# Samples' recurrence moved from the tail into the input projection of a hybrid decoder step

## The chip, the cores and the metric

The kernel runs on one core of a Trainium2 chip. The metric is the device time of one execution in microseconds. Engines: TensorE (PE, its weight loads PEld), VectorE (DVE), ScalarE (ACT), GpSimd (POOL) and SyncE (SP), which here only issues DMAs; each has its own instruction queue and they wait for one another by semaphores. Sixteen DMA engines serve the core.

## The reference

One layer of a decoder step, in float32, for a prompt of 2048 tokens and for 8 sequences with 4 new tokens each (32 "samples"; 2080 columns in all). `h = rmsnorm(x)`, then `z = h @ w_in`, whose columns feed four mixers; their gated outputs go through `w_out` and a last RMS norm.

- A: attention with forget gates; for the samples over 64 cached pages of 128 keys per sequence.
- B: a matrix-state recurrence (RWKV-7), 4 heads of 64, followed by a group norm, a bonus and a gate.
- C: causal pooling. D: a convolution of width 31 with layer norm and a pointwise product.

The part that is moved is B's recurrence for the samples, for each of the 8 sequences from its own 64x64 state per head, four tokens one after another:

```
def rwkv7_step(s, inp):
    r_t, w_t, k_t, v_t, kk_t, a_t = inp
    s_kk = jnp.einsum('bhvk,bhk->bhv', s, kk_t)
    s = s * w_t[:, :, None, :] - s_kk[..., None] * (kk_t * a_t)[:, :, None, :] + v_t[..., None] * k_t[:, :, None, :]
    o = jnp.einsum('bhvk,bhk->bhv', s, r_t)
    return s, o
```

Behind it, for all 2080 columns: `o = ((o - mean) * rsqrt(var + GN_EPS)) * gn_g + gn_b`, plus `sum(r * k * rk) * v`, times a gate; the mean and the variance run over each head's 64 rows.

## The kernel before

Everything is laid out with channels on the 128 partitions and tokens along the free dimension. Five queues are written out by hand. The order of the work:

1. **Input projection** (lines 753 to 757 are its chunk): 25 slots of 128 output columns, each in 5 chunks of 416 tokens (`CHUNKS`, `CW`) of 8 matmuls, in PSUM banks 0 to 4. ScalarE evicts each chunk, and the slot is stored to `zT` in DRAM. Beside it VectorE and GpSimd do the mixers C and D and B's preparation, with small matmuls in banks 5 to 7. At slot 22 B's preparation is over: `smp` holds the samples' columns of r, decay, k, kk, rate and v (6 x 2 x 32 per partition), and eight DMAs (`rw_stored`) have stored the prompt's parts.
2. After slot 23 TensorE computes the **value rows** (L841, banks 5 to 7, 17 tiles), ScalarE copies them to `vtok`. Then slot 24. VectorE computes the log forget gates from `vtok` (L1757 to L1776, `nl_ready`, `nc_ready`); TensorE turns them (L738) between chunks 0, 1 and 2 of slot 24.
3. SyncE meanwhile loads `wvf`, masks, `aux` (L479 to L483) and then `kq`, `qT_s`, `kT_s` (L488 to L490) for the attention, waits for `nc_ready`, writes `ncD` and loads its broadcast. GpSimd gathers the cached forget rows into `scores_`.
4. **Prompt attention** (L895, L908, L919), until about 1153 us.
5. **Prompt's scan** (`rwkv_pair`, matmuls by the helper at L948): 8 pairs, in each of them four `key_step`s of the samples' attention, whose 16 pages of 128 KB each SyncE issues one by one (L525). Ahead of the third set of pages SyncE loads an identity `id64_s` (L541), behind it the samples' states `s_wkv` (L545).
6. **The tail.** VectorE: `s_done` comes after four steps of the samples' recurrence. Each step first spreads five of the samples' quantities (columns with channels on partitions) into block-diagonal tiles `z_exp` (L2029); TensorE multiplies each by `ones_head` (L1194), so that in PSUM every partition has the whole row of its head; then VectorE updates the state (L2034 to L2054). TensorE turns two blocks of the samples' attention probabilities per step (`turn_probs`, L738), and ScalarE copies them back (L1526). Then the **group norm**: 30 sums over heads (L1242) in the order t (channel half), c (chunk) with a `value_tile` after every third; VectorE subtracts the mean (L2068), ScalarE squares, takes logarithm and exponential for the inverse root, VectorE multiplies the bonus (L2075), and when all is there it scales (L2083) and applies gain, bonus, bias and gate over whole halves of 2080 columns (L2086, L2087, `mixb_ready` 2). A value tile is 8 small matmuls over 1 MB of cached values that GpSimd gathers (L720) into one of four slots, `v_slot`; the next gather into a slot waits for the tile that used it.
7. **Output projection** (`project`, L1257): 17 token tiles, each 2 x 8 matmuls of 512 columns, with the other 54 value tiles in between, residual and RMS norm behind.

In the group norm a wait for the loads of `g_rkk`, `g_v` and `gate_b` (`gn_in`, six DMAs of 1 MB issued when the scan is over, L558 to L561) and for `s_done` stands ahead of the first sum.

Of the kernel before, what the change touches and what calls it, by code (L numbers as in the profile page):

```python
# [11 lines left out]
P = 128  # L12
# [14 lines left out]
COL_VF, VF = 512, 260  # L27
MIX_A, MIX_B, MIX_C, MIX_D = 0, 2, 4, 6
# [21 lines left out]
CH = 64  # L50
# [35 lines left out]
def build(nc, I, O):  # L86
    ctx = ExitStack()
    with ctx:
# [7 lines left out]

        ncD = nc.dram_tensor("ncD", [4, SEQ], F32, kind="Internal").ap()
# [165 lines left out]
        dmask = area(HT + 24402, P)  # L263
# [79 lines left out]
        id64_s = area(HT + 12932, CH)  # L343
        wkv_o = area(7200, 256)[0:CH]
        s_wkv = area(15616, DEC_BATCH, 2 * 64)
        z_exp = area(0, 5, DEC_BATCH * 2 * 64)
        s_tmp = area(5120, DEC_BATCH * 2 * 64)
        s_tm2 = area(6144, DEC_BATCH * 2 * 64)
        s_kk = area(7168, 16)
# [16 lines left out]
        s_z = sem("s_z")  # L366
        s_mm2 = sem("s_mm2")
# [84 lines left out]
        def _(sp):  # L452
# [124 lines left out]
            sp.wait_ge(s_done, 1)  # L577
            for t in range(2):
                sp.dma_start(O['wkv_sample'][:, 0, 2 * t:2 * t + 2].rearrange("b h v k -> (h v) b k"),
                             s_wkv[:, :, t * 64:(t + 1) * 64]).then_inc(wkv_stored, 16)  # L580
# [8 lines left out]
            sp.wait_ge(mixb_ready, 2)  # L589
# [145 lines left out]
        def _(pe):  # L735
# [97 lines left out]
            def value_rows(n):  # L833
                r = P if n < TT else SMP
                if n == 0:
                    pe.wait_ge(pars_in, 32)
                    pe.wait_ge(lora_read, 20)
# [4 lines left out]
                last.then_inc(vf_mm, 1)  # L842

# [18 lines left out]
            for n in range(2, N_SLOTS):  # L862
# [13 lines left out]
                if n == 18:  # L876
                    loras()
                if n == 23:
# [320 lines left out]
            pe.wait_ge(D['pT'], D0['pT'] + 16)  # L1199
            pe.wait_ge(D['p'], D0['p'] + 9)  # L1200
            transpose(psum[0:SMP, 6, 0:P], s_new[:, :]).then_inc(D['pT_tr'], 1)
            pe.wait_ge(D['l_bc'], D0['l_bc'] + 1)
            nc.tensor.matmul(psum[:, 7, 0:P], l_bc[:, :], ident[:, :], start=True, stop=True).then_inc(D['l_mm'], 1)

# [22 lines left out]
            pe.wait_ge(s_done, 1)  # L1227
            pe.wait_ge(gn_in, 16 * 6)
            pe.wait_ge(D['pT'], D0['pT'] + 17)
            g = 0  # L1230
            for k, src in enumerate((o_rw, gn_sq, g_rkk)):
                for t in range(2):
                    for c in range(CHUNKS):
# [11 lines left out]
                        if g % 3 == 0:  # L1245
                            value_tile(g // 3 - 1)
# [973 lines left out]
```

## Time and profile before

| | us |
|---|---|
| median of 3 runs | 1962.89 (1961.5 to 1963.37) |
| the profiled execution | 1961.91 |
| its span in the profile | 1960.1 |
| TensorE busy | 1801.5 (92%) |
| VectorE busy | 817.9 (42%) |
| ScalarE busy | 478.5 (24%) |
| GpSimd busy | 170.1 (9%) |

The profile is one execution. Its span runs from the first to the last instruction, and the device time is 1.8 us more. Times of the rows are microseconds from the start of the span. The chain of waits is followed back from the last instruction: at each step to what released it. The granted clock is a share of TensorE's full speed, and the DMA share is the busy share of the 16 DMA engines.

### The profile page before, as it was taken

The page shows a single profiled execution, that of the slowest core. Times are in us where ns is not written, and L with a number is a line of the kernel's source. Part 1 is how long each engine was busy: PE and PEld are TensorE (multiplying, and loading weights), DVE is VectorE, ACT ScalarE, POOL GpSimd, SP SyncE. Part 2 cuts the span into 40 slices and gives each one's busy share as a digit, 9 for nine tenths or more (in the row PEclk, how much of TensorE's full clock was granted, in tenths as well). Part 3 has the DMA queues.
Part 4 walks back from the last instruction along what each step waited for, and adds up shares of the span by engine and source line. Part 5 has one row for each costly group of instructions (what it writes and reads, how often), then busy time and mean ns, then how long its engine had stood idle before and what let it go on. Part 6 is the DMA issues. An engine that isn't in the chain of part 4 may idle for free.

```text
span 1960.1 us, 34623 instructions
## 1 busy us (share of the span) xinstructions
PE 1801.5 (92%) x14642; PEld 1092.4 (56%) x14642; DVE 817.9 (42%) x1662; ACT 478.5 (24%) x855; POOL 170.1 (9%) x220
## 2 busy tenths in 40 slices
PE   6999999999999999979999997887788786999997
PEld 3555555555554556746776775666667342444442
DVE  4450799732213350036556533444434864111112
ACT  4301100010526231125554531111112231100000
POOL 1000000011000005600000000000000001111110
PEclk9999999999999999989999998998989798999999
DMA  6222321385230535141100057777776536878782
GB/s 224 78 105 80 118 87 64 121 196 158 92 120 33 204 153 206 50 152 39 54 1 1 2 175 224 221 236 218 213 226 193 226 100 230 296 272 277 277 297 74
DMA packets 149269, 298.62 MB, mean 152 GB/s; under 512 B 23301, under 2 KB 119349, under 8 KB 130742
## 3 DMA queue, kind: packets, MB, share of 16 engines
q1 hardware_dynamic: 126602, 152.65, 24.7%
q0 software_dynamic: 18240, 115.82, 17.3%
q10 hardware_dynamic: 4272, 27.93, 3.6%
q8 instruction: 116, 1.90, 0.4%
q14 instruction: 39, 0.32, 0.1%
HBM read 234.66 MB, written 63.92 MB: 152 GB/s over the span
## 4 chain that ended last, share of the span: by engine, by line
PE 58%; DVE 17%; SPq 15%; issue 4%; DMA 3%; ACT 3%; POOL 0%; ACTq 0%; DVEq 0%
PE psum L756 23%; PE psum L1257 12%; SPq L525 12%; DVE big L1647 8%; PE psum L908 6%; PE psum L948 4%; PE psum L841 3%; PE psum L919 3%; PE psum L895 2%; SPq L521 2%; PE psum L788 1%; ACT big L1326 1%; PE psum L1242 1%; DMA rkv<-big 1%; DVE big L2029 1%
## 5 line engine op out<-in xcount | busy, mean ns | idle before, releaser
L756 PE MATMUL psum<-big,wbuf 128*128 128x416 f32 x1920 | 675.4, 513 | 3.9 <-DVE big L1577 3.4
L756 PEld LDWEIGHTS psum<-big,wbuf 128*128 128x128 f32 x1920 | 365.0, 190 | 310.7 <-issue 309.0
L948 PE MATMUL psum<-big 64*64 64x64 f32 (+2 forms) x6496 | 269.6, 281 | 48.8 <-DMA big<-in_k_pages 34.0
L948 PEld LDWEIGHTS psum<-big 64*64 64x64 f32 (+1 forms) x6496 | 190.0, 132 | 140.1 <-issue 69.5
L1295 ACT ACTIVATE zst<-psum 128x416 f32<-128x416 f32 x125 | 64.0, 516 | 540.7 <-PE psum L756 540.6
L1257 PE MATMUL psum<-big 128*128 128x512 f32 (+1 forms) x408 | 181.8, 595 | 0.0
L720 POOL DMA_INDIRECT big<-in_cache_v,pidx x64 | 60.7, 949 | 1027.2 <-PE psum L948 1020.5
L1647 DVE SCALAR_TENSOR_TENSOR big<-big,pars 128x2048 f32<-128x2048 f32 x120 | 148.2, 1298 | 1.1
L1257 PEld LDWEIGHTS psum<-big 128*128 128x128 f32 (+1 forms) x408 | 76.2, 187 | 101.4 <-issue 101.4
L2116 DVE TENSOR_TENSOR zst<-zst,psum 128x1024 f32<-128x1024 f32 (+1 forms) x17 | 20.7, 1221 | 224.5 <-PE psum L1257 224.5
L1555 ACT ACTIVATE big<-zst 128x1024 f32<-128x1024 f32 (+1 forms) x17 | 18.0, 1057 | 299.8 <-DVE zst L2116 299.8
L1257 PE MATMUL psum<-wbuf,big 128*128 128x512 f32 (+1 forms) x136 | 70.1, 639 | 16.7 <-DVE big L2091 15.5
L895 PE MATMUL psum<-big 64*128 64x512 f32 (+3 forms) x320 | 73.8, 568 | 6.0 <-DVE big L1801 5.1
L908 PE MATMUL psum<-big 128*128 128x128 f32 x544 | 72.3, 285 | 7.1 <-DVE big L1827 6.6
L908 PE MATMUL psum<-big,zst 128*128 128x128 f32 x544 | 72.2, 285 | 5.9 <-DVE big L1827 5.4
L919 PE MATMUL psum<-wbuf,big 128*64 128x128 f32 x544 | 77.0, 282 | 0.0
L919 PE MATMUL psum<-big 128*64 128x128 f32 x544 | 77.0, 282 | 0.0
L908 PEld LDWEIGHTS psum<-big 128*128 128x128 f32 x544 | 64.8, 193 | 16.5 <-DVE big L1827 8.7
L908 PEld LDWEIGHTS psum<-big,zst 128*128 128x128 f32 x544 | 64.7, 193 | 15.3 <-issue 7.0
L919 PEld LDWEIGHTS psum<-wbuf,big 128*64 128x64 f32 x544 | 57.7, 137 | 25.6 <-issue 17.1
L1438 ACT COPY wbuf<-psum 128x512 f32<-128x512 f32 (+3 forms) x80 | 41.5, 518 | 120.3 <-PE psum L908 120.3
L720 POOL DMA_INDIRECT big<-in_logf_rows,lidx x64 | 60.5, 945 | 34.7 <-issue 19.2
(238 smaller groups left out, 1818.2 us busy)
## 6 DMA issues: line engine op xcount, KB each, us to landing
big<-in_k_pages SPq DMA_DIRECT2D x352, 128.0 KB, 2.3
zT<-zst ACTq DMA_DIRECT2D x25, 1040.0 KB, 6.5
zst<-in_k_pages SPq DMA_DIRECT2D x160, 128.0 KB, 2.4
wbuf<-in_w_slots SPq DMA_DIRECT2D x24, 512.0 KB, 4.5
big<-zT POOLq DMA_DIRECT2D x11, 1024.0 KB, 5.6
rwS<-big POOLq DMA_DIRECT2D x8, 1024.0 KB, 4.2
big<-rwS SPq DMA_DIRECT2D x8, 1024.0 KB, 5.9
zst<-in_x_prompt SPq DMA_DIRECT2D x16, 512.0 KB, 9.2
```

Of the source, the lines that this page charges most:

```text
L525: sp.dma_start(k_ring[k % NRING][:, n % DEC_BATCH, n // DEC_BATCH, :, :], I['k_pages'][bass.ds(page, 1)].rearrange("o p r c -> (o p) r c") ...
L720: g.indirect_dma_start(out=dst, out_offset=None, in_=cache, in_offset=bass.IndirectOffsetOnAxis(ap=idx, axis=0)).then_inc(s, 16)
L756: last = nc.tensor.matmul(psum[:, m % CHUNKS, 0:CW], w[:, k, :], hT[:, k, c * CW:(c + 1) * CW], start=(k == 0), stop=(k == KT - 1))
L841: last = nc.tensor.matmul(psum[0:r, 5 + n % 3, 0:VF], hT[:, k, n * P:n * P + r], wvf[:, k, :], start=(k == 0), stop=(k == KT - 1))
L895: last = nc.tensor.matmul(psum[:, 2 * (b % 2) + h, 0:w], kq[hs, 1, pr, i * P:(i + 1) * P], kq[hs, 0, pr, c * 512:c * 512 + w], start=True, ...
L908: last = nc.tensor.matmul(psum[:, 4 + h, k * P:(k + 1) * P], rows_[j % 2][h][:, x:x + P], diag[:, j % 2, h, :], start=True, stop=True)
L919: last = nc.tensor.matmul(psum[h * 64:h * 64 + 64, 6 + j % 2, 0:P], vtok[:, k, (2 * pr + h) * 64:(2 * pr + h + 1) * 64], probsT[h][:, k * ...
L948: return nc.tensor.matmul(out, l, r, start=start, stop=stop, skip_group_check=True)
L1257: last = nc.tensor.matmul(psum[0:n, 2 * u + o, :], l, wo[e][:, o * 512:(o + 1) * 512], start=(k == 0), stop=(k == 7))
L1295: nc.scalar.activation(zst[:, u, c * CW:(c + 1) * CW], psum[:, m % CHUNKS, 0:CW], f, scale=0.125 if n in (QA, QA + 1) else 1.0).then_inc(z ...
L1438: nc.scalar.copy(probsT[h][:, c * 512:c * 512 + width(j, c)], psum[:, 4 + h, 0:width(j, c)]).then_inc(pT_ready, 1)
L1647: last = v.scalar_tensor_tensor(out, in_, w, out, ALU.mult, ALU.add)
```

## The change

- **The samples' recurrence** moves to step 1 and 2 above. After slot 22 TensorE turns the ten 128x32 column tiles of `smp` (`turn_samples`) into PSUM banks 5 to 7, VectorE copies them to `z_turned` (two copies of 32 x 640, `z_kept`), and SyncE stores them as rows in DRAM (`zsD`, four DMAs). Then SyncE loads for each step five rows into `z_row`, each load a broadcast of two rows of 1024 values to 64 partitions each; the load of a row for the next step waits for the row's use in this one. VectorE runs the four steps from SBUF, ahead of the forget gates' work, with one subtraction moved off the state. The outputs go to `o_smp` and are copied to `o_rw` in the scan. The value rows now also wait for `z_kept`.
- In **SyncE's queue** this stands between the load of `aux` and those of `kq`, `qT_s`, `kT_s`: the two loads of the states, the stores and row loads, a wait for `s_done`, and the stores of the new states with a wait. The two state loads, the identity's load and a wait leave the scan.
- **Group norm** right behind the scan: TensorE waits only for `gn_in`; sums in the order c, t; `turn_probs` 0 and 1 after the first ten sums, 2 to 7 after all thirty, then the new keys' part and ten value tiles without anything between. VectorE applies gain, bonus, bias and gate by chunk (`mixb_ready` up to 10).
- **Output projection**: branch B's two products come last of each eight and wait for their chunks.

```
+        z_row = [area(HT + 13010 + n * 1024, 1024) for n in range(5)]
+        s_wkv = area(HT + 18130, DEC_BATCH, 2 * 64)
...
...
# on SyncE
             for u in range(2):
                 sp.wait_ge(z_stored[u], 16 * (11 - u))
             for t in range(2):
+                sp.dma_start(s_wkv[:, :, t * 64:(t + 1) * 64],
+                             I['state_wkv'][:, 0, 2 * t:2 * t + 2].rearrange("b h v k -> (h v) b k")).then_inc(s_in, 16)
+            sp.wait_ge(z_kept, 2)
+            for i in range(DEC_SEQ):
+                sp.dma_start(zsD[i].rearrange("m h (b x) -> b (m h) x", x=P), z_turned[i::DEC_SEQ].rearrange("b m h x -> b (m h) x")).then_inc(zs_stored, 16)
+            sp.wait_ge(zs_stored, 16 * DEC_SEQ)
+            for i in range(DEC_SEQ):
+                for n, m in enumerate(Z_ORDER):
+                    if i > 0:
+                        sp.wait_ge(s_used, 5 * (i - 1) + n + 1)
+                    sp.dma_start(z_row[n], zsD[i, m].unsqueeze(1).to_broadcast([2, 64, 1024])).then_inc(x_in[n], 16)
+            sp.wait_ge(s_done, 1)
+            for t in range(2):
+                sp.dma_start(O['wkv_sample'][:, 0, 2 * t:2 * t + 2].rearrange("b h v k -> (h v) b k"),
+                             s_wkv[:, :, t * 64:(t + 1) * 64]).then_inc(wkv_stored, 16)
+            sp.wait_ge(wkv_stored, 32)
+            for t in range(2):
                 for m, first in ((0, KA), (1, QA)):
                     sp.dma_start(kq[:, m, t, :], zT[first + t]).then_inc(kq_in, 16)
...
-            sp.dma_start(id64_s, I['rw_masks'][:, 3 * CH:4 * CH]).then_inc(s_in, 16)
             key_pages(2)
-            sp.wait_ge(mixa_stored, 32)
-            for t in range(2):
-                sp.dma_start(s_wkv[:, :, t * 64:(t + 1) * 64],
-                             I['state_wkv'][:, 0, 2 * t:2 * t + 2].rearrange("b h v k -> (h v) b k")).then_inc(s_in, 16)
...
# on TensorE
+            def turn_samples():
+                pe.wait_ge(made, IDENT)
+                pe.wait_ge(s_dec, 1)
+                pe.wait_ge(L_ready, 6)
+                pe.wait_ge(lora_read, 20)
+                for n in range(10):
+                    last = transpose(psum[0:SMP, 5 + n // 4, n % 4 * P:n % 4 * P + P], smp[:, n // 2, n % 2, :])
+                last.then_inc(z_tr, 1)
...
+                if n == 22:
+                    turn_samples()
...
-            for i in range(DEC_SEQ):
-                for n in range(5):
-                    k = i * 5 + n
-                    pe.wait_ge(s_z, k + 1)
-                    if k >= 3:
-                        pe.wait_ge(s_used, k - 2)
-                    for hf in range(2):
-                        last = nc.tensor.matmul(psum[:, 2 * (k % 3) + hf, :], ones_head[:, :],
-                                                z_exp[:, n, hf * 512:(hf + 1) * 512], start=True, stop=True)
-                    last.then_inc(s_mm2, 1)
-                turn_probs(2 * i)
-                turn_probs(2 * i + 1)
...
-            pe.wait_ge(s_done, 1)
             pe.wait_ge(gn_in, 16 * 6)
-            pe.wait_ge(D['pT'], D0['pT'] + 17)
             g = 0
             for k, src in enumerate((o_rw, gn_sq, g_rkk)):
-                for t in range(2):
-                    for c in range(CHUNKS):
+                for c in range(CHUNKS):
+                    for t in range(2):
...
-                        if g % 3 == 0:
-                            value_tile(g // 3 - 1)
+                if k == 0:
+                    turn_probs(0)
+                    turn_probs(1)
+            for blk in range(2, 8):
+                turn_probs(blk)
...
+            for n in range(10):
+                value_tile(n)
...
-                for k, e in enumerate((2, 3, 0, 1, 4, 5, 6, 7)):
+                for k, e in enumerate((0, 1, 4, 5, 6, 7, 2, 3)):
+                    if k == 6 and o == 0:
+                        pe.wait_ge(mixb_ready, 2 * ((T * P + n - 1) // CW + 1))
...
# on VectorE, ahead of its wait for vf_evac
+            for i in range(DEC_SEQ):
+                k = i * 5
+                kk_row, decay_row, rate_row, k_row, r_row = z_row
+                vcol = smp[:, 5].rearrange("p t (b i) -> p b t i", i=DEC_SEQ)[:, :, :, i].unsqueeze(3).to_broadcast([P, DEC_BATCH, 2, 64])
+                dve.wait_ge(x_in[0], X_SEEN[0] + 16 * (i + 1))
+                v.tensor_tensor(s_tmp, S, kk_row, ALU.mult).then_inc(s_used, 1)
+                dve.wait_ge(s_used, k + 1)
+                ch.link(v.reduce_sum(s_kk[:, :], bt(s_tmp), AX.X))
+                dve.wait_ge(x_in[1], X_SEEN[1] + 16 * (i + 1))
+                v.tensor_tensor(S, S, decay_row, ALU.mult).then_inc(s_used, 1)
+                dve.wait_ge(x_in[2], X_SEEN[2] + 16 * (i + 1))
+                v.tensor_tensor(bt(s_tmp), bt(rate_row), s_kk[:, :].unsqueeze(2).to_broadcast([P, BT, 64]), ALU.mult).then_inc(s_used, 1)
+                dve.wait_ge(x_in[3], X_SEEN[3] + 16 * (i + 1))
+                v.tensor_tensor(s_tm2.rearrange(b4, b=DEC_BATCH, t=2), k_row.rearrange(b4, b=DEC_BATCH, t=2), vcol, ALU.mult).then_inc(s_used, 1)
+                dve.wait_ge(s_used, k + 4)
+                ch.link(v.tensor_tensor(s_tm2, s_tm2, s_tmp, ALU.subtract))
+                ch.link(v.tensor_tensor(S, S, s_tm2, ALU.add))
+                dve.wait_ge(x_in[4], X_SEEN[4] + 16 * (i + 1))
+                v.tensor_tensor(s_tmp, S, r_row, ALU.mult).then_inc(s_used, 1)
+                dve.wait_ge(s_used, k + 5)
+                ch.link(v.reduce_sum(s_kk[:, :], bt(s_tmp), AX.X))
+                ch.link(v.tensor_copy(o_smp[:, :, :].rearrange("p t (b i) -> p b t i", i=DEC_SEQ)[:, :, :, i],
+                                      s_kk[:, :].rearrange("p (b t) -> p b t", t=2)))
+            dve.sem_inc(s_done, 1)
```

## Rows read from the trace of the kernel before

**Rows 1.** The page, busy times of the engines over the span

```profile
PE 1801.5 (92%) x14642; PEld 1092.4 (56%) x14642; DVE 817.9 (42%) x1662; ACT 478.5 (24%) x855; POOL 170.1 (9%) x220
```

**Rows 2.** Chain of waits in order of time, 1500 to 1650: start, length, what

```profile
1504.51 2.60 DMA big<-in_k_pages
...
1526.40 5.76 DVE big L2029 x5
...
1543.61 5.76 DVE big L2029 x5
...
1630.96 2.61 DVE big L2083 x5
```

**Rows 3.** Groups by line on VectorE, 1526 to 1596: count, busy, mean ns

```profile
L2029 DVE TENSOR_TENSOR big<-smp,big 128x1024 f32<-128x1024 f32 x20 | 23.1, 1218 | 0.1
L2049 DVE TENSOR_TENSOR big<-big 128x1024 f32<-128x1024 f32 x4 | 4.9, 1226 | 0.1
```

**Rows 4.** Timeline of TensorE, 1590 to 1650: start, length, last the idle before

```profile
1591.97 1.14 PE L738 MATMUL psum<-ident,big 128*128 128x128 f32 x8 [1.25 <-ACT big L1526]
...
1596.22 3.66 PE L1242 MATMUL psum<-big,ones_head 128*128 128x416 f32 x6
...
1604.34 2.36 PE L1242 MATMUL psum<-big,ones_head 128*128 128x416 f32 x6
1606.63 1.07 PE L948 MATMUL psum<-big 128*32 128x256 f32 x16
...
1646.83 3.75 PE L1257 MATMUL psum<-wbuf,big 128*128 128x512 f32 x4 [15.54 <-DVE big L2091]
```

**Rows 5.** Timeline of VectorE, 726 to 830

```profile
748.26 0.06 DVE L1755 MEMSET big<- 128x4 f32 x1
824.69 0.23 DVE L1757 TENSOR_TENSOR big<-big 128x68 f32<-128x68 f32 x1 [76.36 <-ACT big L1326]
```

**Rows 6.** Line 561, the loads of the gate rows for the group norm

```profile
L561 SPq DMA_DIRECT2D big<-zT x2: 430/458/485, 1527.9 to 1529.6; - x2
...
DMA to landing us min/median/max: 9.4/12.6/15.8
```

**Rows 7.** Line 720, gathers of cached values, 1500 to 1960

```profile
DMA to landing us min/median/max: 5.4/7.5/11.2
```

**Rows 8.** Windows: busy of PE, PEld, DVE, ACT, POOL, clock, DMA share, GB/s

```profile
1530.00:1545.00 15.00, 10.86 (x35) 5.46 (x34) 14.66 (x14) 8.13 (x17) 0.00 (x0) 0.93 1.01 418
...
790.00:820.00 30.00, 30.00 (x138) 25.79 (x137) 0.00 (x0) 3.10 (x8) 22.69 (x25) 1.00 0.16 53
```

**Rows 9.** Timeline of SyncE's queue in the scan

```profile
1182.40 1.06 SPq L545 DMA_DIRECT2D big<-in_state_wkv  x2
```

**Rows 10.** Timeline of TensorE, 730 to 860

```profile
764.05 60.12 PE L841 MATMUL psum<-big 128*128 128x260 f32 x272
...
829.80 1.47 PE L738 MATMUL psum<-ident,big 128*4 128x128 f32 x12
...
837.35 17.03 PE L756 MATMUL psum<-big,wbuf 128*128 128x416 f32 x48
```

**Rows 11.** DMA issues: count, KB each, median us to landing

```profile
big<-zT SPq DMA_DIRECT2D x6, 1040.0 KB, 12.6
...
big<-ncD SPq DMA_DIRECT2D x1, 1024.0 KB, 8.2
...
out_wkv_sample<-big SPq DMA_DIRECT2D x2, 256.0 KB, 3.2
```

**Rows 12.** Window inside the shift rows' transfer (L512), columns as in rows 8

```profile
942.50:942.80 0.30, 0.30 (x4) 0.04 (x2) 0.00 (x0) 0.28 (x2) 0.00 (x0) 1.00 0.44 67
```

**Rows 13.** DMA queue q1, 1645 to 1653 (final_norm_g) and 708 to 716 (slot weights)

```profile
q1 hardware_dynamic: 144, 0.52, 20.3%
...
q1 hardware_dynamic: 144, 0.52, 25.9%
```

**Rows 14.** Window in the first output projection, columns as in rows 8

```profile
1651.00:1651.50 0.50, 0.50 (x2) 0.27 (x1) 0.00 (x0) 0.00 (x0) 0.00 (x0) 0.50 0.00 0
```

More of the change, by code:

```diff
@@ L27 @@
 COL_VF, VF = 512, 260
+Z_ORDER = (3, 1, 4, 2, 0)
+X_SEEN = (32, 16, 16, 16, 32)
 MIX_A, MIX_B, MIX_C, MIX_D = 0, 2, 4, 6
@@ L365, in build @@
         s_dec = sem("s_dec")
-        s_z = sem("s_z")
-        s_mm2 = sem("s_mm2")
+        z_tr = sem("z_tr")
+        z_kept = sem("z_kept")
+        zs_stored = sem("zs_stored")
         s_used = sem("s_used")
@@ L836, in value_rows @@
                     pe.wait_ge(pars_in, 32)
-                    pe.wait_ge(lora_read, 20)
+                    pe.wait_ge(z_kept, 2)
                 if n >= 3:
@@ L1244, in _ @@
                         g += 1
-                        if g % 3 == 0:
-                            value_tile(g // 3 - 1)
+                if k == 0:
[3 more added lines that the diff above has]
+                turn_probs(blk)
+            pe.wait_ge(D['pT'], D0['pT'] + 16)
+            pe.wait_ge(D['p'], D0['p'] + 9)
+            transpose(psum[0:SMP, 6, 0:P], s_new[:, :]).then_inc(D['pT_tr'], 1)
+            pe.wait_ge(D['l_bc'], D0['l_bc'] + 1)
+            nc.tensor.matmul(psum[:, 7, 0:P], l_bc[:, :], ident[:, :], start=True, stop=True).then_inc(D['l_mm'], 1)
+            pe.wait_ge(D['pT'], D0['pT'] + 17)
+            for n in range(10):
+                value_tile(n)
             pe.wait_ge(gn_read, 20)
-            pe.wait_ge(mixb_ready, 2)
             pe.wait_ge(D['li'], D0['li'] + 1)
@@ L1408, in _ @@
                         decay((n - 20) // 2 * 3 + c + 1)
+                    if n == 22 and c == 1:
+                        a_(smp[:, 1], smp[:, 1], ACT.Exp, s_dec)
             act.wait_ge(rw_stored, 64)
@@ L1521, in _, with probs_turned @@
             nc.scalar.activation(s_new[:, :], s_new[:, :], ACT.Exp, bias=neg_m[:, :], accum_out=l9[:, 8:9]).then_inc(D['p'], 1)
-            for blk in range(8):
+            def probs_turned(blk):
                 act.wait_ge(D['pT_tr'], D0['pT_tr'] + blk + 1)
@@ L1755, in _, with bt @@
             v.memset(vtok[:, TT, 256:VF], 0.0).then_inc(f_pad, 1)
+            dve.wait_ge(z_tr, 1)
+            turned = psum[0:SMP, 5:8, :].rearrange("p a b -> p (a b)")[:, 0:1280].rearrange("p (m t h k) -> p m t h k", m=5, t=2, h=2)
+            for h in range(2):
+                v.tensor_copy(z_turned[:, :, h, :].rearrange("p m (t k) -> p m t k", t=2), turned[:, :, :, h, :]).then_inc(z_kept, 1)
+            BT = DEC_BATCH * 2
+            b4 = "p (b t k) -> p b t k"
+            def bt(x):
+                return x.rearrange("p (n k) -> p n k", n=BT)
@@ L2056, in _ @@
-            dve.wait_ge(R['o'], TT)
-            dve.sem_inc(s_done, 1)
+            pieces = [(t, slice(c * CW, (c + 1) * CW)) for c in range(CHUNKS) for t in range(2)]
+            for g, (t, cs) in enumerate(pieces):
+                dve.wait_ge(gn_mm, g + 1)
+                v.scalar_tensor_tensor(o_rw[:, t, cs], psum[:, g % 4, 0:CW], -1.0 / 64, o_rw[:, t, cs], ALU.mult, ALU.add).then_inc(gn_read, 1)
+            for g, (t, cs) in enumerate(pieces, 4 * CHUNKS):
+                dve.wait_ge(gn_mm, g + 1)
+                v.tensor_tensor(g_v[:, t, cs], psum[:, g % 4, 0:CW], g_v[:, t, cs], ALU.mult).then_inc(gn_read, 1)
@@ L2060, in _ @@
             v.tensor_scalar(l_bc[:, :], ones_a[:, :], l1[:, :], None, ALU.mult).then_inc(D['l_bc'], 1)
[L2063 to L2076 removed]
             dve.wait_ge(gn_read, 4 * CHUNKS)
             dve.wait_ge(gn_in, 16 * 6)
[L2079 to L2082 removed]
+            for c in range(CHUNKS):
+                cs = slice(c * CW, (c + 1) * CW)
+                dve.wait_ge(gn_root, 2 * c + 2)
+                for t in range(2):
                     ch.mark(v.tensor_tensor(o_rw[:, t, cs], o_rw[:, t, cs], gn_inv[:, t, cs], ALU.mult))
                 ch.join()
[L2085 to L2087 removed]
+                for t in range(2):
+                    ch.mark(v.scalar_tensor_tensor(o_rw[:, t, cs], o_rw[:, t, cs], par[:, t, PGG:PGG + 1], g_v[:, t, cs], ALU.mult, ALU.add))
+                ch.join()
+                for t in range(2):
+                    v.scalar_tensor_tensor(o_rw[:, t, cs], o_rw[:, t, cs], par[:, t, PGB:PGB + 1], gate_b[:, t, cs], ALU.add, ALU.mult).then_inc(mixb_ready, 1)
             dve.wait_ge(D['l_mm'], D0['l_mm'] + 1)
```

125 lines of the change are left out of this document (28 added, 97 removed).

## The prediction

> **What bounds the kernel now.** I read the page first. TensorE is busy for 92% of the span [rows 1], so nearly any gap on it is worth something, and the question is where its gaps are. The chain of waits shows it: the end runs over TensorE through most of the program, over SyncE's issue of key pages in the state scan up to 1504, and between 1526 and 1646 over VectorE [rows 2]. There are two VectorE stretches. From 1526.4 to 1595 it is the samples' recurrence: four steps of 17.2 us (1526.40 to 1543.61), each with five spreads of 1.15 us and then nine operations of 1.22 us and a small copy [rows 2, 3]. From 1630.96 to 1646.8 it is the end of the group norm, after TensorE's 30 head sums and ten value tiles; TensorE idles 15.5 us there before its first output projection [rows 2, 4]. Everything from 1646.8 on is TensorE at full work.
>
> The change takes the recurrence out of that tail and puts it at 738, in the input projection. There VectorE is idle for 76 us, from 748.3 to 824.7 [rows 5]. So the change has two sums: what the tail loses, and whether the recurrence is over before 824.7.
>
> **The tail, without the recurrence.** The clock starts at the same 1526.4. TensorE now goes straight to the group norm and first waits for all six group norm loads. SyncE issues them from 1526.8; the last, a gate row, is issued at 1529.56 and lands 15.8 us later, at 1545.4 [rows 6]. Before, the recurrence hid this wait; now it is 19 us of idle TensorE. Then:
> - Ten head sums with VectorE's subtraction behind each: before, 1596.2 to 1608.4 with three value tiles of 1.07 us in between, so 9 us [rows 4]. 1554.5.
> - Two blocks of probabilities turned at 2.4 us each (1.14 of transposes and 1.25 of wait for ScalarE's copy), and about 1 us until ScalarE has done its last square: 5.8 us [rows 4]. 1560.
> - Twenty more sums: three sums took 2.36 us, 0.79 each, 15.7 us, and ScalarE's change of function about 1 us [rows 4]. 1577.
> - Six blocks turned, 14.4 us, and the new keys and the row of sums as before (1591.97 to 1596.22, less a block), 1.9 us [rows 4]. 1593.
> - Ten value tiles, now in a row. The first four wait in their slots and take 1.07 us each. The gather of the fifth is issued after the first tile, at 1594, and takes a landing of 7.5 us (median; the shortest is 5.4) [rows 7]: 1601.5. The other five come at the DMA engines' pace, 1 MB in 2.5 us (at 418 GB/s, all 16 engines busy [rows 8]) to 3.4 us (the pace of before, a tile every 2.36 + 1.07), 3.0 taken: 1616.5, and the last tile ends at 1617.6.
>
> VectorE's own normalization, thirty operations of 0.6 us from 1577 on (five took 2.61 [rows 2]), is over at 1595 and hides under this; so do the weights and the first rows of the residual. Projection starts at 1617.6 in place of 1646.8: **29.2 us gained**. Bounds: 24 (tiles at 3.4 us, 3 us of matmuls at the lower clock after the wait) to 34 (2.5 us, landing 5.4). The order of the eight products in a tile changes no count; the 16 tiles behind are TensorE-bound and keep their pace.
>
> In the scan SyncE issues the key pages without a pause, and it loses the two loads of the states (1.06 us) and that of the identity (half of that) [rows 9]: **1.6 us gained**. The exponential that leaves ScalarE's queue at the scan's start and the copy of the samples' outputs (0.2 us) lie beside that issue: 0, and at most 0.5 us if they did not.
>
> **The recurrence in the projection.** TensorE turns the samples' columns after slot 22: one slot, 28 us (80 instructions of 0.355; 48 took 17.03), before the value rows begin at 764.05, so at 736; ten transposes at 0.12 us (twelve took 1.47) [rows 10], 1.3 us. VectorE gets to them when its index operations end at 748.3 [rows 5], and copies 2 times 32x640 out of PSUM, 640/1024 of 1.22 us or 0.8 us each. z_kept at 750. TensorE asks for it at 765.4: hidden. SyncE then issues four stores (0.5 us each [rows 9]) and waits for them (the state stores, of more bytes, landed in 3.2 us [rows 11]): the first row load is issued at 755.3 and moves data some 2 us later, at 757.3. SyncE's queue also holds, behind the whole recurrence, the state stores and the loads of kq, qT_s and kT_s.
>
> A step on VectorE is nine operations of 1.22 us and a copy: 11.3 us, four are 45 us, and if the rows were always there it would end at 805. So all depends on the twenty row loads of 512 KB. Each spreads two source rows of 4 KB over 64 partitions each: its source counts 2 x 64 x 1024, with 2 as the outermost dimension. All the broadcasts of before have 128 outermost. One transfer of before has a short outer dimension: the shift rows at 939.8, 7 x 128 x 33. Alone on the engines, it held a DMA share of 0.44 while it was in full flow, which is 7 of 16 engines [rows 12]. I conclude that a transfer is cut along its outermost dimension, and that a row load will run on 2 of the 16 engines.
>
> That row has 7 on both sides; a row load has 2 on the source's side and 128 partitions on the other, and no row tells which side counts. But a share must begin at the same element on both sides, and sixteen shares of eight partitions begin inside the source's two entries; I give two engines 85%. The Trainium skill (DMA: Bandwidth & Descriptors, Why a DMA increments its semaphore by 16 and not by 1) says that the engines used are the largest number up to 16 that divides the slowest dimension of both sides. By that rule it is two, and the sum below stands; by the other reading of the row, all sixteen, it is the first rival.
>
> Price of a row load on two engines: 64 packets of 4 KB on each. The nearest transfer is the broadcast of final_norm_g, the same 512 KB in the same packets on 16 engines: 20.3% of 16 engines over 8 us are 26 engine-us for 144 packets, 0.18 us a packet, 11.6 us for 64 [rows 13]. Sixteen engines in full flow moved 418 GB/s, 26 each, which makes 10.0 us (the lower bound) [rows 8]. The slot weights took 25.9% of 8 us, 33 engine-us, or 0.23 us a packet beside other traffic: 14.7 us (the upper bound) [rows 13]. A stream of twenty without pauses is nearer to full flow: 10.5 us taken. Five loads are in flight at a time and VectorE needs a row for only 1 to 3 us, so the two engines never run dry, and the sum is 20 x 10.5 = 210 us. Until 825 the gathers of the forget rows take 0.16 of every engine [rows 8]: +11 us. The last product, reduction and copy: 2.7 us. The recurrence ends at 757.3 + 221 + 2.7 = **981**.
>
> **What is then late.** VectorE's chain for the forget gates, at 824.69 before [rows 5], is behind it: 156.3 us late. TensorE runs the value rows and the first chunk of slot 24, then stands at the turn of the forget rows (829.8 before, 986 now) [rows 10]; the transposes' 1.3 us vanish in that wait. After it the clock is at its lower level: in the first projection the granted clock was 0.50 (1.2 of 2.4 GHz) until 1651.5, 4.6 us after TensorE had begun again [rows 14]; the same here costs 2.3 us. SyncE issues the state stores at 981 (landing 3.2), then the kq loads, which need 12.6 us and some 4 of issue [rows 11]: there at about 1002, while TensorE asks for them behind slot 24, at 855 + 156 = 1011 [rows 10]. Hidden, by 9 us. The order behind (ncD, its broadcast) only moves.
>
> **Sum** against the profiled execution (1961.9 us around a span of 1960.1, 1.0 under the median): +156.3 + 2.3 - 29.2 - 1.6 = +127.8. **2091 us** for the median.
>
> **Rivals.**
> 1. *The row loads use all 16 engines* (the partitions' side counts). Then a load costs 26 engine-us / 16 = 1.6 us, the recurrence is VectorE's 45 us and ends at 805, 20 us before VectorE is wanted; kq lands at 825, 30 us early. Only the transposes' 1.3 us stay: 1962.9 - 29.2 - 1.6 + 1.3 = 1933 (1926 to 1940). This is the case on the other side, and it decides below 3.2 us a load (65 us for twenty) fully, and up to 4.8 us (a delay of 31 us) as a gain. For it: every other broadcast ran so. Against it: the 0.44 of the shift rows. 12%.
> 2. *All engines, but the repeated reads of one row are slow.* The first broadcast of ncD took 8.2 us for 1 MB with little beside it [rows 11]. Half of that is 4.1 us a load, the recurrence ends at 842, 17 us late: 1950. 3%.
> 3. *Two engines at the weights' packet time.* 14.7 us a load: 294 + 11 us, an end at 1065, 84 us later than forecast: 2175. For it: two engines read the same 4 KB again and again, and the ncD broadcast was slow. Against it: the broadcast of final_norm_g, also of one 4 KB row, had 0.18 us a packet. 10%.
>
> **The numbers.** The forecast has 75%. With rival 3 that is 85% for a loss; its own range is 2070 (10.0 us a load and no contention: 200 in place of 221 us) to 2175. Outside I leave rivals 1 and 2, 15%; the tail's bounds add 5 us on either side, and the low end, nearer to the rivals I leave out, 9 more: 2055 to 2180. What can be told from no change is 0.2%, 4 us; no case lies there but a row load of just 4.8 us: 1%. Faster 14%, slower 85%.
>
> **What would show it.** Right: during the row loads a DMA share near 2/16 = 0.13 plus the gathers' 0.16, falling to 0.13 after 825; VectorE waiting for them from 757 to 981 with some 45 us of work; TensorE idle from 832 to 986; then a tail with 19 us idle at 1526 + 156, six value tiles at about 3 us, and the projection 30 us sooner after the scan. Wrong: row loads landing in 3 us and no gap at 832 (rival 1), a landing of 15 us each (rival 3), or, in the tail, value tiles that no longer wait for DMA.

## The result and the profile after

The changed kernel takes **2083.5 us** (median of 4 runs, 2082.5 to 2089.5) beside 1963.1 us of the kernel before (1961.5 to 1964.2): a ratio of 1.062 with a 95% interval of 1.060 to 1.064. It is 6% slower; forecast were 2091 us (2055 to 2180). The profiled execution has a span of 2080.7 us, 120.6 more than the one of before.

From its page: the busy times, the chain by engine (SPq is SyncE's queue of DMA issues, "issue" is time in which an engine waited for nothing that the profile shows) and one group of DMA issues:

```profile
PE 1768.2 (85%) x14572; PEld 1081.2 (52%) x14572; DVE 799.3 (38%) x1661; ACT 478.3 (23%) x855; POOL 173.3 (8%) x220
...
PE 50%; SPq 15%; DMA 15%; DVE 12%; issue 4%; ACT 3%; POOL 0%; ACTq 0%; DVEq 0%
...
big<-zsD SPq DMA_DIRECT2D x20, 512.0 KB
```

TensorE's busy time is even a little less than before [rows 1], over a longer span: the time went into waiting. The chain runs over DMA for 15% of the span, and over SyncE's queue for another 15%. SyncE's own timeline in the projection (start, duration of the issues, line, tile, count):

```profile
740.33 4.12 SPq L492 DMA_DIRECT2D big<-in_state_wkv  x2
750.55 2.98 SPq L496 DMA_DIRECT2D zsD<-big  x4
755.30 197.45 SPq L502 DMA_DIRECT2D big<-zsD  x20
979.90 1.02 SPq L505 DMA_DIRECT2D out_wkv_sample<-big  x2
983.73 0.81 SPq L510 DMA_DIRECT2D big<-zT  x2
```

VectorE's timeline shows what each of the twenty rows costs (the bracket is the idle time ahead and who ended it):

```profile
770.54 1.23 DVE L1791 TENSOR_TENSOR big<-big 128x1024 f32<-128x1024 f32 x1 [20.02 <-DMA big<-zsD]
...
834.19 1.23 DVE L1791 TENSOR_TENSOR big<-big 128x1024 f32<-128x1024 f32 x1 [9.33 <-DMA big<-zsD]
...
855.05 1.23 DVE L1797 TENSOR_TENSOR big<-big 128x1024 f32<-128x1024 f32 x1 [8.88 <-DMA big<-zsD]
865.22 1.23 DVE L1799 TENSOR_TENSOR big<-big,smp 128x1024 f32<-128x1024 f32 x1 [8.94 <-DMA big<-zsD]
...
977.12 1.23 DVE L1804 TENSOR_TENSOR big<-big 128x1024 f32<-128x1024 f32 x1 [6.48 <-DMA big<-zsD]
```

From the sixth row (834.19) to the twentieth (977.12) are 142.9 us for 14 rows, 10.2 us each, in which VectorE works for some 2.2 us. The windows of both stretches (length, busy time of each engine, granted clock, DMA share, GB/s) say on how many engines:

```profile
757.00:825.00 68.00, 68.00 (x295) 54.31 (x294) 11.21 (x10) 7.24 (x18) 52.15 (x53) 1.00 0.30 107
830.00:975.00 145.00, 1.84 (x6) 0.69 (x4) 30.99 (x27) 0.00 (x0) 2.34 (x3) 0.52 0.13 53
```

In the second window next to nothing else moves: a share of 0.13 is 2 of 16, and 53 GB/s are 26 each, the same as an engine moved in full flow [rows 8]. TensorE pays for it at the turn of the forget rows, and everything behind starts late:

```profile
984.27 2.71 PE L751 MATMUL psum<-ident,big 128*4 128x128 f32 x12 [152.44 <-DVE big L1815]
...
1010.89 0.71 PE L919 MATMUL psum<-big 64*128 64x128 f32 x8 [0.61 <-ACT zst L1311]
```

The kernel before, at its attention and at the last transposes of the scan:

```profile
854.98 0.72 PE L895 MATMUL psum<-big 64*128 64x128 f32 x8 [0.61 <-ACT zst L1295]
...
1524.90 0.60 PE L738 MATMUL psum<-ident,big 128*64 128x128 f32 x2
```

So the attention begins at 1010.9 in place of 855.0: 155.9 us. The tail gives some back. TensorE's timeline from the end of the scan to the first output projection:

```profile
1679.90 0.61 PE L751 MATMUL psum<-ident,big 128*64 128x128 f32 x2
1699.96 9.24 PE L1246 MATMUL psum<-big,ones_head 128*128 128x416 f32 x20 [19.45 <-DMA big<-zT]
...
1727.01 1.06 PE L751 MATMUL psum<-ident,big 128*128 128x128 f32 x8
...
1731.70 1.94 PE L751 MATMUL psum<-ident,big 128*128 128x128 f32 x8 [1.26 <-ACT big L1543]
...
1745.15 5.25 PE L972 MATMUL psum<-big 128*32 128x256 f32 x64
1754.39 1.16 PE L972 MATMUL psum<-big 128*32 128x256 f32 x16 [4.00 <-DMA big<-in_cache_v,pidx]
1757.03 1.93 PE L972 MATMUL psum<-big 128*32 128x256 f32 x16 [1.47 <-DMA big<-in_cache_v,pidx]
...
1768.82 5.44 PE L1273 MATMUL psum<-big 128*128 128x512 f32 x12
```

and the windows of the last four of the six later blocks and of the last value tiles:

```profile
1731.50:1744.40 12.90, 7.77 (x33) 6.29 (x34) 12.65 (x23) 4.35 (x9) 0.00 (x0) 0.50 0.00 1
...
1760.00:1769.00 9.00, 8.24 (x67) 2.44 (x60) 0.42 (x1) 0.00 (x0) 3.01 (x4) 0.51 1.01 418
```

The scan ends 155.0 us after its place in the kernel before (1679.90 beside 1524.90), which is 0.9 us gained, and the projection starts 122.0 us after its place (1646.83 [rows 4]), so the tail gained 33.0 us. With 1.4 us behind it: 155.9 - 0.9 - 33.0 - 1.4 = 120.6.

### The profile page after: what moved, and what is told of

Its sections match the earlier page's. It is cut to its first block, busy times and chain, and to the rows that moved or that the text cites. A ratio compares the mean times of both kernels' runs of the same rounds, so it can differ in the third digit from the quotient of the medians.

```text
span 2080.7 us, 34482 instructions
## 1 busy us (share of the span) xinstructions
PE 1768.2 (85%) x14572; PEld 1081.2 (52%) x14572; DVE 799.3 (38%) x1661; ACT 478.3 (23%) x855; POOL 173.3 (8%) x220
## 4 chain that ended last, share of the span: by engine, by line
PE 50%; SPq 15%; DMA 15%; DVE 12%; issue 4%; ACT 3%; POOL 0%; ACTq 0%; DVEq 0%
PE psum L769 20%; SPq L547 12%; PE psum L1273 12%; DMA big<-zsD 10%; DVE big L1663 7%; PE psum L932 6%; PE psum L972 4%; PE psum L943 2%; PE psum L919 2%; SPq L543 2%; DMA big<-zT 2%; ACT big L1342 1%; PE psum L801 1%; DMA rkv<-big 1%; PE psum L1246 1%
## 5 line engine op out<-in xcount | busy, mean ns | idle before, releaser
L972 PE MATMUL psum<-big 64*64 64x64 f32 (+2 forms) x6496 | 274.3, 284 | 58.0 <-DMA big<-in_k_pages 36.5
L1273 PE MATMUL psum<-big 128*128 128x512 f32 (+1 forms) x408 | 186.1, 606 | 1.1 <-issue 1.1
L751 PE MATMUL psum<-ident,big 128*128 128x128 f32 (+2 forms) x212 | 34.1, 310 | 161.6 <-DVE big L1815 152.4
L751 PEld LDWEIGHTS psum<-ident,big 128*128 128x128 f32 (+2 forms) x212 | 26.1, 158 | 170.4 <-issue 167.2
L1342 ACT ACTIVATE big<-big 128x416 f32<-128x416 f32 (+3 forms) x81 | 59.1, 777 | 168.7 <-DVE big L1811 153.7
L943 PE MATMUL psum<-wbuf,big 128*64 128x128 f32 x544 | 76.9, 282 | 0.0
L943 PE MATMUL psum<-big 128*64 128x128 f32 x544 | 76.9, 282 | 0.0
L932 PEld LDWEIGHTS psum<-big,zst 128*128 128x128 f32 x544 | 64.4, 192 | 14.4 <-issue 6.8
```

The costliest lines, as they stand in the source:

```text
L751: return nc.tensor.transpose(out, in_, ident[0:k, 0:k])
L932: last = nc.tensor.matmul(psum[:, 4 + h, k * P:(k + 1) * P], rows_[j % 2][h][:, x:x + P], diag[:, j % 2, h, :], start=True, stop=True)
L943: last = nc.tensor.matmul(psum[h * 64:h * 64 + 64, 6 + j % 2, 0:P], vtok[:, k, (2 * pr + h) * 64:(2 * pr + h + 1) * 64], probsT[h][:, k * ...
L972: return nc.tensor.matmul(out, l, r, start=start, stop=stop, skip_group_check=True)
L1273: last = nc.tensor.matmul(psum[0:n, 2 * u + o, :], l, wo[e][:, o * 512:(o + 1) * 512], start=(k == 0), stop=(k == 7))
L1342: nc.scalar.activation(out, in_, f, **kw).then_inc(s, 1)
```

## The experiments

The theory: a transfer is cut along its outermost dimension, a row load has 2 there, and its two engines set the 155 us. The rival with the most left for it: reading the same rows of HBM again and again is slow whatever the engines. For the tail: whether the 33 us come from the recurrence's leaving or from the new order. Runs 5, 6, 7 and 12 were made in sessions in which the kernel before took 2035 and 2028 us, all others where it took 1965 us (see experiment 10), so ratios are compared.

**1. The row loads by halves.** Runs 1, 2, 3 and 5 are edits of the changed kernel (11 is 1 again), 4 of the kernel before; 6 builds on 1, and 7, 8, 9 and 12 each on the one named.

```
-sp.dma_start(z_row[n], zsD[i, m].unsqueeze(1).to_broadcast([2, 64, 1024])).then_inc(x_in[n], 16)
+for h in range(2):
+    sp.dma_start(z_row[n][h * 64:(h + 1) * 64], zsD[i, m, h].unsqueeze(0).to_broadcast([64, 1024])).then_inc(x_in[n], 16)
```

> Theory (a transfer is cut along its outermost dimension, 2 for a row load, so 2 of 16 engines carry it at 10.2 us each): each row load is now two transfers of 64 partitions from one source row, outermost dimension 64, so all 16 engines carry it. The recurrence ends at 805 to 810 (four steps of 11.3 us from 759 on), before VectorE is wanted at 824.7, and the gap of 152 us on TensorE is gone: 1963 - 33.0 (tail) - 0.9 (scan) - 1.4 (behind) + 1.3 (ten transposes) = 1929 us. Rival (it is the repeated reads of one row that are slow, 4 us or more per 512 KB whatever the engines): the recurrence ends at 842 or later, 1946 us or more, and if the number of engines plays no part at all, 2083 as with the change.

Measured: 1927.6 us, 0.9817 (0.9793 to 0.9841). The same bytes go to the same partitions, and the gap is gone; VectorE's last copy of the recurrence and TensorE at the turn:

```profile
818.14 0.18 DVE L1808 COPY o_smp<-big 128x16 f32<-128x16 f32 x1
```

```profile
824.67 5.85 PE L770 MATMUL psum<-big,wbuf 128*128 128x416 f32 x16
830.36 1.47 PE L752 MATMUL psum<-ident,big 128*4 128x128 f32 x12
```

TensorE goes from the first chunk of slot 24 (first row) into the turn with no idle time. The recurrence ended some 10 us later than expected, since VectorE still waits 1 to 3 us for some rows, but before it is wanted.

**2 and 3. Four and eight entries in the outermost dimension**, by two and four copies of each row in DRAM (shown for two; with four, `q` runs over 4 and the shape is `[8, 16, 1024]`):

```
+for q in range(2):
+    sp.dma_start(zsD[i, :, :, q].rearrange("m h (b x) -> b m h x", x=P), z_turned[i::DEC_SEQ]).then_inc(zs_stored, 16)
...
+sp.dma_start(z_row[n], zsD[i, m].rearrange("h q x -> (h q) x").unsqueeze(1).to_broadcast([4, 32, 1024])).then_inc(x_in[n], 16)
```

> Each source row is stored twice in HBM and a row load reads the four copies as its outermost dimension, 4 x 32 x 1024, with the same bytes, packets and partitions. Theory: 4 engines, half of 10.2 us a load; 5.9 us while the gathers run (12 loads until 828), 5.1 us after (8 loads), last product 2.7 us: the recurrence ends near 872, 47 us behind the 824.7 of before. 1929 - 1.3 + 47 + 0.6 (clock) + 2 (four more stores) = 1977 us, and a DMA share near 0.25 after 825. Rival (repeated reads slow, engines not the reason): 2083 as with the change, or, if reading two places in place of one helps, something between that does not follow 10.2 / 2.

> Four copies of each row, outermost dimension 8, twelve more stores (6 us). Theory: 8 engines, a quarter of 10.2 us a load, near 2.9 us beside the gathers, 14.7 us a step against VectorE's 11.3: from 763 on the recurrence ends at 820 to 828, at or just behind the 824.7: 1931 us (1929 to 1936). Rival: 2083, or no straight line through the three points 2, 4 and 8.

Measured: 1984.5 us, 1.0108 (1.0085 to 1.0131), and 1947.1 us, 0.9911 (0.9886 to 0.9936). The fourth step of the run with four, on VectorE:

```profile
866.94 1.23 DVE L1798 TENSOR_TENSOR big<-big 128x1024 f32<-128x1024 f32 x1 [3.79 <-DMA big<-zsD]
872.03 1.23 DVE L1800 TENSOR_TENSOR big<-big,smp 128x1024 f32<-128x1024 f32 x1 [3.86 <-DMA big<-zsD]
```

A row takes 5.1 us, half of 10.2. What SyncE's queue of loads moved says the same (packets, MB, share of 16 engines). The changed kernel from 850 to 970:

```profile
q1 hardware_dynamic: 1534, 6.19, 12.8%
```

with four, from 835 to 870:

```profile
q1 hardware_dynamic: 896, 3.57, 25.3%
```

and with eight, from 800 to 825, beside the gathers:

```profile
q1 hardware_dynamic: 1088, 4.20, 44.2%
```

That is 25.2, 25.2 and 23.8 GB/s for each busy engine (6.19 MB in 120 us on 0.128 x 16 = 2.05 engines, and so on), on 2, 4 and, on average, 7 of them. The order is as the theory has it, and so is the price with four; the rival's 2083 us fall. Both times missed the forecasts of 1977 and 1931 us, because the recurrences ended at 879.9 and 845.5 for 872 and at most 828: while the gathers ran a row took 5.9 to 8.8 us with four (5.9 expected) and 3.2 to 7.3 us with eight (2.9 expected). With eight the flow was thinner at first: from 775 to 800 it was 2.78 MB at a share of 39.6%, 17.5 GB/s for each busy engine.

**4. The group norm's part alone, on the kernel before.**

```
-for t in range(2):
-    for c in range(CHUNKS):
+for c in range(CHUNKS):
+    for t in range(2):
...
-        if g % 3 == 0:
-            value_tile(g // 3 - 1)
+for n in range(10):
+    value_tile(n)
...
-for k, e in enumerate((2, 3, 0, 1, 4, 5, 6, 7)):
+for k, e in enumerate((0, 1, 4, 5, 6, 7, 2, 3)):
```

with the waits by chunk and VectorE's end by chunk as in the change.

> Only the group norm's part of the change on the kernel before: sums and normalization in token chunks, the ten value tiles in a row behind the sums, branch B last in each tile; the recurrence and the turning of the probabilities stay in the tail. Theory (the tail's gain of 33 us comes from the recurrence leaving, and the order is nearly even, since the 15.5 us wait for VectorE is replaced by value tiles that wait for their pages): sums from 1596.2 for 9.2 + 14.6 us as with the change, ten tiles in 23.7 us, first projection at 1643.7 in place of 1646.8, 1.4 less behind it: 1958 us, from 1956 to 1963. Rival (the order makes the gain, the 15.5 us wait just goes): 1947 us or less.

Measured: 1963.8 us, 0.9995 (0.9979 to 1.0010), no difference where 1958 us (1956 to 1963) were expected. TensorE's fifth value tile and first projection:

```profile
1630.40 1.93 PE L948 MATMUL psum<-big 128*32 128x256 f32 x16 [5.02 <-DMA big<-in_cache_v,pidx]
...
1644.84 5.42 PE L1258 MATMUL psum<-big 128*128 128x512 f32 x12
```

The projection starts 2.0 us earlier than before, and 4.1 us earlier if both are counted from the end of the scan (117.2 us for 121.3). The 15.5 us wait for VectorE [rows 4] is replaced by value tiles that wait for their pages, so some 29 of the 33 us of the tail are the recurrence's leaving, as far as one trace shows.

**5. Sixteen entries**, eight copies of each row.

> Eight copies of each source row, outermost dimension 16, so 16 engines with a source row of their own each (28 more stores, some 20 us more of issue than the change: the first row lands near 774). The question is why the transfers by halves took 0.22 us and more a packet where two engines took 0.16. Theory S (many engines at one 4 KB row of HBM slow each other): with a copy each the packets are back at 0.16 to 0.18 us, VectorE does not wait, steps of 11.3 us, the recurrence ends at 820, hidden: 1928 us. Theory G (it is the number of engines and the gathers beside them, not the shared row): steps of 14 us as with the halves, an end at 832, 7 us behind the 824.7: 1935 us.

Measured: 2003.1 us, 0.9856 (0.9825 to 0.9887), in a slower session, where TensorE's value rows lasted to 898 and would have hidden either end, so the time decides nothing. What tells the two apart is the flow. The halves, from 765 to 800:

```profile
q1 hardware_dynamic: 1944, 6.37, 73.6%
```

sixteen copies, from 788 to 802:

```profile
q1 hardware_dynamic: 804, 2.91, 85.2%
```

15.5 and 15.2 GB/s per busy engine (14.7 with the halves in the same session as this run: 6.10 MB from 765 to 800 at 73.9%, run 6): a source row for each engine did not bring back the 25.2. Its steps were 16.2, 13.4, 12.1 and 12.0 us beside 17.0, 14.2, 13.9 and 12.9 with the halves, with thinner gathers, so the last ones lie between the 11.3 of theory S and the 14 of its rival G, and from 806 to 825 the flow was 17.5 GB/s. Theory S, that the engines slow each other at one row, is then not the main cause; G named no mechanism, and none is shown.

**6. Probabilities turned while the group norm's loads are under way** (on 1).

```
+for blk in range(8):
+    turn_probs(blk)
...   # new keys, row of sums
 pe.wait_ge(gn_in, 16 * 6)
...   # ScalarE
+    nc.scalar.activation(x, x, ACT.Exp, ...)
+    if blk > 0:
+        probs_turned(blk - 1)
```

> The transfers by halves, and all eight blocks of probabilities, the new keys and the row of sums turned while TensorE waits for the group norm's loads (19.6 us). ScalarE alternates exponential and copies, 2.35 us a block: 1.2 + 19 us, then 2.8 us for the last two, so the sums start some 3.5 us later than before, and the turning behind them (3.5 and 18.1 us) is gone. Theory (the tail is a plain sum of TensorE's stretches, the turning in the wait is free): 1927.6 - 21.6 + 3.5 = 1909 us. Rival (the value tiles' pages or VectorE's normalization then end last, since the tiles come 18 us sooner): VectorE needs 18.5 us from the last sum and the ten tiles 23.7, so at most 1 or 2 us are lost, unless the pages come at the pace of the DMA engines from the same moment as before, which would leave 1920 or more.

Measured: 0.9766 (0.9744 to 0.9788); 1986.3 beside 2034.6 us. From the end of the scan's last transposes to the first projection it is 77.0 us, against 88.9 with the halves (88.3 in the change). 12 of the 18 us came. The turning takes longer than the 2.35 us a block of the expectation:

```profile
1606.94 1.94 PE L752 MATMUL psum<-ident,big 128*128 128x128 f32 x8 [1.25 <-ACT big L1537]
1610.14 1.94 PE L752 MATMUL psum<-ident,big 128*128 128x128 f32 x8 [1.25 <-ACT big L1537]
```

That is 3.2 us a block, with the 1.94 us of transposes that the change's last blocks show at a granted clock of 0.50, so the sums began 28.7 us after the scan and not 23.

**7. The same as 6, with a value tile after every third sum.**

> As the run before, with a value tile after every third sum, as the kernel before the change had it. Theory (a value tile in a row waits for its page, 1.4 us and more each, and one between sums does not): sums and tiles take the 35.2 us that they took before (1596.2 to 1631.4) in place of 23.3 + 23.7 us, and then the first token chunk of VectorE's end is waited for, 4 us: 1909 - 47.0 + 39.2 = 1901 us. Rival (VectorE's end takes the whole gain, as its 15.5 us did before the change, though only the first chunk is waited for): 1909 or more.

Measured: 0.9804 (0.9778 to 0.9831), which is no better than 6, where 1901 of 1963 us were expected. Sums and tiles took 35.7 us (35.2 expected), and then

```profile
1685.70 7.96 PE L1271 MATMUL psum<-big 128*128 128x512 f32 x12 [18.24 <-DVE big L2088]
```

L2088 is not a chunk of the normalization but the reciprocal of the row of sums behind all of it. I had not looked for what else TensorE waits for there.

**8. The reciprocal ahead of the group norm** (on 7).

```
+dve.wait_ge(D['l_mm'], D0['l_mm'] + 1)
+v.reciprocal(li[:, :], psum[:, 7, 0:P]).then_inc(D['li'], 1)
 pieces = [(t, slice(c * CW, (c + 1) * CW)) for c in range(CHUNKS) for t in range(2)]
```

> The interleaved tail, with VectorE's reciprocal of the row of sums, which TensorE also waits for before the first projection, moved from behind the normalization to ahead of the group norm (its input is there then). In the run before, TensorE stood 18.2 us for it after the last value tile. Theory (that reciprocal's place was the whole wait; the first token chunk is done 4 us after the last sum and only the last two products of a tile need it): the projection starts right behind the last value tile, 18 us sooner than in the interleaved run and 12.6 us sooner after the scan than with the tiles in a row: 1927.6 - 11.9 (measured from the end of the scan to the projection, halves against turning first) - 12.6 = 1903 us where the kernel before takes 1963, a ratio of 0.9695. Rival (the chunks of VectorE's end are the limit): TensorE waits for them tile by tile, up to 16 us in all, and the ratio stays at 0.977.

Measured: 1926.5 us, 0.9795 (0.9768 to 0.9821), where 0.9695 was expected. From scan to projection it is 68.6 us in place of 82.7, but two other waits come up, for weights that SyncE issues after the twentieth sum, and for VectorE's copy of the first sequence's values, again behind the normalization:

```profile
1600.80 7.85 PE L1271 MATMUL psum<-big 128*128 128x512 f32 x12 [4.41 <-DMA big<-in_w_out]
...
1619.57 1.03 PE L973 MATMUL psum<-big 128*128 128x16 f32 x4 [8.20 <-DVE big L2095]
```

The halves alone give the same time (run 11, in the same session): there scan to projection is 88.0 us, 19.4 more, but from the projection to the end of the program it is 311.9 us, and here 324.5.

**9. Two pairs of PSUM banks for the turned blocks** (on 8; TensorE waits for the copies one block later, and ScalarE reads from the same pairs).

```
-transpose(psum[:, 6 + j // 4, ...
+transpose(psum[:, 6 - 2 * (blk % 2) + j // 4, ...
```

> The same, and the turned blocks go to two pairs of PSUM banks in turn, so that TensorE turns a block while ScalarE copies the last one. A block took 3.2 us (1.94 of transposes at a granted clock of 0.50 and 1.25 of wait). Theory: the period is then ScalarE's exponential and two copies, 1.13 + 0.1 + 1.07 = 2.3 us; 8 x 0.9 = 7 us less, of which the loads of the group norm (19.6 us after the scan) leave 5: 1898 us where before takes 1963, 0.967. Rival (the loads of the group norm land later under the denser queue, or the lower clock makes the sums slower): as the run before.

Measured: 1911.8 us, 0.9711 (0.9682 to 0.9740). The expectation was 0.967. Two blocks now take 4.3 us, and scan to projection is 56.2 us, 12.4 less than in 8 where 5 were expected: the sums begin 8.4 us sooner, their first three take 2.4 us and not 4.3, and the wait for the weights is 2.1 us shorter. The wait for the values' copy is still there:

```profile
1538.02 4.07 PE L752 MATMUL psum<-ident,big 128*128 128x128 f32 x16 [0.59 <-ACT big L1541]
...
1606.57 1.04 PE L973 MATMUL psum<-big 128*128 128x16 f32 x4 [9.32 <-DVE big L2095]
```

**10. The kernel before once more**, for its trace.

> The kernel before itself, for its trace on the chip of these runs. On the chip of the last three runs every kernel was 70 us slower and the before took 2035 us; in two traces the matmuls of the value rows from 773 to 845 came 2.8 us apart with nothing waited for. If this is a property of that chip and not of the edits, the kernel before shows the same there; on the first chip (1963 us) it shows them without a pause.

Measured: 1965.3 us, in a session in which the kernel before took 1965 us, so not in a slower one as the expectation wanted. Its value rows run without a pause:

```profile
769.50 60.12 PE L841 MATMUL psum<-big 128*128 128x260 f32 x272
```

In the traces of the slower sessions (runs 5, 6, 7 and 12) the same 272 matmuls take 124 to 130 us. Some 25 of them come 1 to 4 us apart until about 845, the others close together. One such row, in run 6:

```profile
776.61 0.46 PE L855 MATMUL psum<-big 128*128 128x260 f32 x1 [1.80 <-issue]
```

These 64 to 70 us are as much as the kernel before is slower in those sessions (63 to 70 us). That it loses them at the same place was not seen, since no trace of it was taken there. Whether this belongs to a chip is not shown either: the session of runs 1 to 4 and the slower one of runs 5 to 7 bear the same chip number. What holds back the issue stays open.

**11. The halves again**, beside 8 and 9.

> The transfers by halves again, on the same chip as the two runs above, so that their differences hold: ratio 0.9817 as before on a chip of 1963 us, about 0.982 on one of 2035.

Measured: 1928.7 us, 0.9796 (0.9766 to 0.9827), as the first time.

**12. The first values kept before the normalization** (on 9).

```
+dve.wait_ge(D['pv_mm'], D0['pv_mm'] + DT)
+v.tensor_copy(pv[:, :], psum[:, 4, 0:256]).then_inc(D['pv'], 1)
 dve.wait_ge(gn_read, 4 * CHUNKS)
```

> The run with two pairs of banks, and VectorE's copy of the first sequence's values (0.42 us, its eight tiles are done by then) moved ahead of the normalization's thirty operations. In the run before, TensorE stood 9.3 us for that copy at the first combination, after the first output tile. Theory (that copy's place was the whole of this wait): 1911.8 - 9.3 = 1902.5 us, a ratio of 0.967. Rival (VectorE's last chunks or the residual's sum take its place at the second or third tile, since VectorE ends its normalization 18 us after the last sum and a tile takes 9 us): some 3 to 9 us of waits come back, 1906 us or more, 0.969 to 0.971.

Measured: 0.9711 (0.9695 to 0.9727), 1971.9 beside 2028.3 us, where 0.967 was expected and 0.969 to 0.971 by its rival. The wait for that copy is gone from the trace, and from the start of the first output tile to that of the third it is 20.1 us, not 30.8:

```profile
1662.65 8.09 PE L1271 MATMUL psum<-big 128*128 128x512 f32 x12 [3.70 <-DMA big<-in_w_out]
...
1682.76 5.42 PE L1271 MATMUL psum<-big 128*128 128x512 f32 x12
```

but scan to projection took 60.1 us, 3.9 more than in 9. From the end of the scan to the end of the program it is 374.3 us for 381.5 in 9. It saves 56.4 us against its own before and run 9 saved 54.0 against its own, so the 9 us less were not confirmed in the times. Runs 9 and 12 beat both kernels; between them the ratios decide nothing.

## Why the prediction was right

- **The row loads use two engines.** Right: the share is 0.13, and the price of a row falls from 10.2 to 5.1 us as the source's outermost dimension goes from 2 to 4. The partitions' side had 128 all along and brought no engine. The Trainium skill (DMA: Bandwidth & Descriptors, Why a DMA increments its semaphore by 16 and not by 1) has this rule, the largest number up to 16 that divides the slowest dimension of both sides; the shares here agree with it for 2 (0.13) and 4 (0.25).
- **A row costs 10.5 us, and 11 us for the gathers.** It cost 10.2 us, and the gathers more than 11: the first six rows took 76.9 us from 757.3 on, 15.7 over their 61.2. The two misses nearly cancel, by luck: 219.8 us for 221, and an end at 979.8 for 981.
- **When the first is issued**: 755.3, as worked out.
- **What is late**: the forget gates by 155.3 us (156.3), the attention by 155.9, where the sum had 158.6. The lower clock cost 1.5 us, not 2.3: after the idle stretch, at a granted clock of 0.50 from 984 to 987, twelve transposes took 2.71 us in place of 1.47, and the next chunk 5.98 in place of 5.75. And the sum had left out a slack: in the kernel before, TensorE came to this turn some 0.8 us after VectorE was ready, so it now begins only 154.5 us later (984.27 beside 829.80 [rows 10]).
- **kq and its neighbours hidden**: right; TensorE goes into the attention with 0.61 us of idle time, as in the kernel before.
- **The scan**: 0.9 us gained, 1.6 forecast.
- **The tail**: 33.0 gained, 29.2 forecast, inside the bounds of 24 to 34. The first two turns took 3.5 us and not 5.8 (ScalarE's squares were hardly late), the other twenty sums 14.5 and not 16.7; the six later blocks took 17.4 for 14.4, since four of them ran at half clock (0.50 granted), which I had not allowed for; the new keys and the row of sums took 0.8 for 1.9, and the value tiles 23.7 for 24.6. So the tail came out right partly because misses of both signs cancel. 1.4 us of gain came behind, which the sum did not have.
- **Rival 1** (all engines) is what runs 1 and 11 build, and they give 1928 and 1929 us for the 1933 that it named. **Rival 2** (repeated reads slow) is not what bounds the change, but something of the kind shows when 16 engines take part: 15.5 GB/s each are 2.1 us a row at best where the rival had 1.6 for all engines. It stays below the 3.2 us from which it would matter. **Rival 3** (0.23 us a packet) fell: 10.2 us for 64 packets are 0.16.

So the loss is one transfer's shape. With the loads by halves the same move gains 1.8 to 2.0%.

## What to carry to other kernels

Before a broadcast or a strided load is put on a path that someone waits for, count its outermost dimension on both sides: a `[2, 64, 1024]` source is 128 partitions wide and still runs on 2 of 16 engines, and two DMAs of `[64, 1024]` cured it here. In the profile it showed as a DMA share of k/16 (0.13 and 0.25) with full GB/s per busy engine. And when a wait is taken out of a tail, look at everything that is queued behind the long block on each engine: here a reciprocal of 0.95 us and a copy of 0.42 us held TensorE for 18 and 9 us, one after the other.

## What the runs showed that was not expected

The row loads are slow when all engines take part: 15.5 GB/s per busy engine with one source row for all, 15.2 with a copy for each, while two or four engines had 25.2 with next to nothing beside them and the value gathers 26 on all sixteen (418 GB/s). The source may be part of it: with nothing beside them, the broadcast of `final_norm_g`, one row of 4 KB, had 20 GB/s per busy engine [rows 13], and that of `ncD`, with packets of 2 KB, 14 (1.05 MB at 47.3% of 10 us). But the traffic beside is a rival. The gathers of the forget rows slow down too: 0.10 us of an engine's time for a packet in the kernel before (768 packets at 16.1% of 30 us), 0.14 with the halves (849 at 21.8% of 35 us). And with eight engines the flow was 17.5 and then 23.8 GB/s, beside gathers both times. The small region of HBM, the broadcast, the few packets that each engine gets of one transfer (four with the halves, eight with sixteen copies) and the traffic beside were not separated.
